# The feed-forward down projection of a decoder layer: seven products of half blocks in place of eight

## The reference, cut to what matters

```
y = (silu(c[..., :D_FF]) * c[..., D_FF:]) @ lp['ffn_w_down']    # 1056 x 2816 times 2816 x 1024
x = x + rms_norm(y, norm_g[5])                                  # over the 1024 columns of a row
```

## Time and profile before

| | |
|---|---|
| median of three runs | 3142.71 us (3140.87 to 3143.19) |
| span of the profiled execution | 3141.0 us |
| PE busy over the span | 2918.1 us (93%) |
| DVE, ACT, POOL busy | 1244.7, 631.2, 465.4 us |
| DMA | 345.05 MB, mean 110 GB/s |

### The profile page before, as it was taken

The page is one execution under the profiler, slowest core; times in us unless marked ns, Lnnn a source line. Parts: engine busy times, 40 slices in busy tenths (PEclk is TensorE's granted clock), DMA queues, the critical chain, the costliest instruction groups (busy, mean ns, idle before and its releaser), DMA issues. The chain is left out here.

```text
span 3141.0 us, 42970 instructions
## 1 busy us (share of the span) xinstructions
PE 2918.1 (93%) x15234; PEld 2006.5 (64%) x15234; DVE 1244.7 (40%) x2937; ACT 631.2 (20%) x1523; POOL 465.4 (15%) x349
## 2 busy tenths in 40 slices
PE   7999999998999788889999799998799999989998
PEld 5777777765666555456666566555588888864443
DVE  3111123233542567246666334233465655640000
ACT  2101100001222243134444211244211111110000
POOL 0000000003320333100000100011223333310100
PEclk8999999999999899989999899899899999999999
DMA  7544264426972542541111453300233334322110
GB/s 175 114 99 94 48 189 142 129 86 180 274 228 73 170 128 74 173 128 39 37 41 48 154 169 138 110 34 27 84 115 126 127 113 140 103 86 99 37 38 23
DMA packets 339366, 345.05 MB, mean 110 GB/s; under 512 B 61177, under 2 KB 310201, under 8 KB 337806
## 3 DMA queue, kind: packets, MB, share of 16 engines
q1 hardware_dynamic: 299458, 262.80, 29.1%
q10 hardware_dynamic: 39734, 79.98, 7.6%
HBM read 289.37 MB, written 110.01 MB: 127 GB/s over the span
## 5 line engine op out<-in xcount | busy, mean ns | idle before, releaser
L284 PE MATMUL d_ps<-d_w,mixer_u_T 128*128 128x288 f32 (+2 forms) x2048 | 585.5, 433 | 16.1 <-PEq L145 10.3
L284 PEld LDWEIGHTS d_ps<-d_w,mixer_u_T 128*128 128x128 f32 x2048 | 382.8, 194 | 157.0 <-issue 39.9
L288 PE MATMUL d_ps<-mixer_u_T,d_w 128*128 128x352 f32 x1152 | 402.6, 488 | 27.0 <-ACT d_ob L308 17.5
L2978 PE MATMUL down_ps<-down_w,feed_g_T 128*128 128x512 f32 x704 | 305.2, 596 | 8.4 <-DMA down_w<-ffn_w_down 8.4
L288 PEld LDWEIGHTS d_ps<-mixer_u_T,d_w 128*128 128x128 f32 x1152 | 212.2, 198 | 151.8 <-issue 70.6
L2978 PEld LDWEIGHTS down_ps<-down_w,feed_g_T 128*128 128x128 f32 x704 | 134.5, 191 | 177.5 <-issue 168.3
L3188 PE MATMUL ffn_ps<-up_u_T,up_up_w 128*128 128x264 f32 x704 | 164.6, 393 | 3.8 <-DMA ffn_state<-state_ffn_conv 3.8
L3188 PE MATMUL ffn_ps<-ffn_T,up_up_w 128*128 128x264 f32 x704 | 163.8, 386 | 0.0
L3188 PE MATMUL ffn_ps<-up_u_T,ffn_S 128*128 128x264 f32 x704 | 163.8, 386 | 0.0
L308 DVE COPY d_ob<-d_ps 128x288 f32<-128x288 f32 (+3 forms) x144 | 66.4, 462 | 244.2 <-PE d_ps L284 164.4
L3188 PEld LDWEIGHTS ffn_ps<-up_u_T,up_up_w 128*128 128x128 f32 x704 | 133.4, 192 | 26.9 <-issue 4.2
(11 more groups left out here) (493 smaller groups left out, 3740.5 us busy)
## 6 DMA issues: line engine op xcount, KB each, us to landing
out_dil_sample<-cache_dil_w ACTq DMA_DIRECT2D x10, 3264.0 KB
up_up_w<-ffn_w_up SPq DMA_DIRECT2D x44, 512.0 KB, 5.2
cmp_rows<-cache_nsa_kv SPq DMA_DIRECT2D x128, 128.0 KB
graw<-d_ob SPq DMA_DIRECT2D x72, 176.0 KB
mix_gate<-graw SPq DMA_DIRECT2D x24, 528.0 KB, 6.1
dils_qb<-proj SPq DMA_DIRECT2D x24, 512.0 KB, 7.3
d_w<-w_in SPq DMA_DIRECT2D x24, 512.0 KB, 5.6
ssd_x<-proj SPq DMA_DIRECT2D x29, 384.0 KB, 4.9
```

The costliest lines, as they stand in the source:

```text
L284: mm = pe.matmul(self.ps[u % 2][0:rows, 0:cols], self.u_T[:, k, r0:r0 + rows], self.view(i)[:, k, :], start=(k == 0), stop=(k == DK - 1))
L288: mm = pe.matmul(self.ps[u % 2][:, 0:cols], self.view(i)[:, k, x, :], self.u_T[:, k, c * third:(c + 1) * third], start=(k == 0), stop=(k = ...
L2978: mm = pe.matmul(ps[i % ring][:, 512 * h:512 * (h + 1)], lhs_T[:, k, r0:r0 + m], w[:, k, 512 * h:512 * (h + 1)], start=(k == 0), stop=(k = ...
```

## The change

The matrix of activations A (1024 tokens x 2816 features) and the weight B (2816 x 1024) are each seen as two by two blocks: A11 is the first 512 tokens by the first 11 feature blocks, B12 the first 11 feature blocks by the second 512 columns. Strassen's scheme in Winograd's form makes the four blocks of the product from seven block products instead of eight, with sums of blocks ahead of and behind them. A block product is 4 half products (one for each 128 tokens), each 11 matmuls of 128 x 512.

- DVE makes eight sums of blocks in place, each in two pieces of 5 and 6 feature blocks (L3102): in A21, A11, A12 and again A11; in B12 (twice), B11 and B21.
- PE's order is P1 into the four banks X, P2 into the banks Y, P5 into Y, P3 added onto P5 in Y, P6 added onto P1 in X, P4 into Y, P7 added onto X. The samples are multiplied with the whole, unchanged B inside P2, before the first sum in B.
- ACT copies P1, P5, P5+P3 and P4 out of PSUM (L3076, L3083, L3086, L3093), into `top`, into the freed block A21 and into the freed block B12. DVE adds the other part from PSUM to each (L3108, L3150, L3158, L3159), and the sum of squares is then taken from SBUF.
- The prompt tiles end in another order: tiles 0 to 3 behind P6, tiles 4 to 7 behind P7. Their residual rows are loaded into freed blocks behind P3.
- The weight comes in eight pieces of half rows (2 KB) instead of five of whole rows (4 KB).

More of the change, by code:

```diff
@@ L2907, in project_down, with after @@
 def project_down(nc, lhs_T, weight, gain_row, x_rows, out_rows, ident, rows_out):
[L2911 to L2914, removed]
+    KH, HALF, C, PAIRS = FFK // 2, D // 2, D // 4, PT // 2
+    SAMPLES = PT
+    EARLY = 5
+    ORDER = ([("P1", p) for p in range(PAIRS)] + [("P2", 0), ("P2", 1), ("P2", 2), ("samples", 0), ("P2", 3)]
+             + [(m, p) for m in ("P5", "P3", "P6", "P4", "P7") for p in range(PAIRS)])
+    OUTS_IN_ORDER = [SAMPLES] + list(range(PT))
+    n = len(OUTS_IN_ORDER)
+    def after(m, p=PAIRS - 1):
+        return ORDER.index((m, p)) + 1
     with Stage(nc, "down") as st:
@@ new lines, in quarters, with kept, bottom, x_of @@
+        def quarters(ap):
+            return ap.rearrange("p (a c) -> p a c", c=P)
+        def kept(part, p):
+            return A("A21", 4 * part, 4 * part + 4, P * p, P * (p + 1))
+        def bottom(p):
+            return w[:, 2 * p:2 * p + 2, HALF:D]
+        junk = A("A21", KH - 2, KH)
+        def x_of(t):
+            p = t % PAIRS
+            return A("A12", 2 * p, 2 * p + 2) if t < PAIRS else B("B22", 2 * p, 2 * p + 2)
+        def y_of(t):
+            return top[:, t] if t < PAIRS else bottom(t - PAIRS)
@@ L2935, in chunks, with halves @@
+        def halves(rows):
+            return rows.rearrange("t (a c) -> t a c", a=2)
         def chunks(rows):
             return rows.rearrange("t (c j) -> c t j", j=C)
[L2938 to L2944, removed]
         with nc.Block() as block:
@@ L2964, in _ @@
-                store(sp, n - 1)
-                for s in range(2):
-                    sp.wait_ge(stored[s], 16 * len(range(s, n, 2)))
+                sp.wait_ge(added, 1)
+                sp.dma_start(chunks(out_rows(SAMPLES)), y_s[:, :]).then_inc(stored, 16)
+                sp.wait_ge(product, after("P3"))
+                for t in range(PAIRS):
+                    sp.dma_start(x_of(t), halves(x_rows(t))).then_inc(xt_in, 16)
+                sp.wait_ge(T_made, 4)
+                for t in range(PAIRS, PT):
+                    sp.dma_start(x_of(t), halves(x_rows(t))).then_inc(xb_in, 16)
@@ L2968, in _ @@
+                for t in range(PT):
+                    sp.wait_ge(added, t + 2)
+                    sp.dma_start(halves(out_rows(t)), y_of(t)).then_inc(stored, 16)
+                sp.wait_ge(stored, 16 * n)
             @block.tensor
             def _(pe):
[L2970 to L2975, removed]
-                    else:
[L2977 to L2999, removed]
+                def half_product(bank, lhs, rhs, p, start):
+                    for k in range(KH):
+                        mm = pe.matmul(bank[:, :], lhs[:, k, P * p:P * (p + 1)], rhs[:, k, :], start=(start and k == 0), stop=(k == KH - 1), skip_group_check=not start)
+                    mm.then_inc(product, 1)
@@ new lines, in _ @@
+                for i in range(len(cuts["B11"]) - 1):
+                    pe.wait_ge(w_in["B11", i], 16)
+                    for k in range(cuts["B11"][i], cuts["B11"][i + 1]):
+                        for p in range(PAIRS):
+                            mm = pe.matmul(X[p][:, :], A("A11")[:, k, P * p:P * (p + 1)], B("B11")[:, k, :], start=(k == 0), stop=(k == KH - 1))
+                            if k == KH - 1:
+                                mm.then_inc(product, 1)
+                for i in range(len(cuts["B21"]) - 1):
+                    pe.wait_ge(w_in["B21", i], 16)
@@ new lines, in _ @@
+                for p in range(3):
+                    half_product(Y[p], A("A12"), B("B21"), p, True)
+                pe.wait_ge(w_in["B12", 0], 16)
+                pe.wait_ge(w_in["B22", 0], 16)
+                for k in range(FFK):
+                    for c in range(4):
+                        mm = pe.matmul(sample_bank[c * NS:(c + 1) * NS, 0:C], lhs_T[:, k, SEQ:TOK], w[:, k, c * C:(c + 1) * C],
+                                       start=(k == 0), stop=(k == FFK - 1))
+                mm.then_inc(product, 1)
@@ new lines, in _ @@
+                pe.wait_ge(S_made, 6)
[6 more added lines that the diff above has]
+                    half_product(X[p], A("A11"), B("B12"), p, False)
+                pe.wait_ge(T_made, 8)
+                for p in range(PAIRS):
+                    pe.wait_ge(held53, p + 1)
+                    half_product(later_bank(p), A("A22"), B("B21"), p, True)
@@ L3001, in _ @@
+                pe.wait_ge(S_made, 8)
+                for p in range(PAIRS):
+                    pe.wait_ge(c12, p + 1)
+                    half_product(X[p], A("A11"), B("B11"), p, False)
             @block.scalar
             def _(act):
[L3003 to L3009, removed]
@@ L3011, in root, with square @@
                 def root(i):
                     act.wait_ge(meaned, i + 1)
[L3013 to L3019 removed]
+                    act.activation(ss[:, 2, i:i + 1], ss[:, 1, i:i + 1], ACT.Sqrt).then_inc(rooted, 1)
+                def square(i, made, count):
+                    act.wait_ge(made, count)
+                    act.activation(junk, y_of(i - 1), ACT.Square, accum_out=ss[:, 0, i:i + 1]).then_inc(squared, 1)
+                    root(i)
@@ new lines, in _ @@
+                act.wait_ge(rows_out, 32)
+                for p in range(PAIRS):
+                    act.wait_ge(product, after("P1", p))
+                    act.copy(top[:, p, 0, :], X[p][:, :]).then_inc(held1, 1)
+                act.wait_ge(product, after("samples", 0))
+                act.activation(y_s[:, :], sample_bank[:, 0:C], ACT.Square, accum_out=ss[:, 0, 0:1]).then_inc(squared, 1)
+                root(0)
+                act.wait_ge(S_made, 4)
+                for p in range(PAIRS):
+                    act.wait_ge(product, after("P5", p))
+                    act.copy(kept(0, p), quarters(later_bank(p)[:, :])).then_inc(held5, 1)
@@ new lines, in _ @@
+                for p in range(PAIRS):
+                    act.wait_ge(product, after("P3", p))
+                    act.copy(kept(1, p), quarters(later_bank(p)[:, :])).then_inc(held53, 1)
+                for p in range(PAIRS):
+                    if p >= 1:
+                        act.wait_ge(squared, 1 + p)
+                    square(1 + p, c12, p + 1)
+                for p in range(PAIRS):
+                    act.wait_ge(product, after("P4", p))
+                    act.copy(bottom(p)[:, 0, :], later_bank(p)[:, :]).then_inc(held4, 1)
@@ L3028, in _ @@
                 dve.tensor_copy(fold[:, 1:4, :], fold[:, 0, :].unsqueeze(1).broadcast_to([P, 3, NS])).then_inc(folded, 1)
-                dve.wait_ge(gain_in, 80)
[L3030 to L3044, removed]
+                two(A("A21"), A("A21"), A("A22"), ALU.add, S_made)
@@ new lines, in _ @@
+                dve.wait_ge(S_made, 2)
+                dve.wait_ge(product, after("P1"))
+                two(A("A11"), A("A21"), A("A11"), ALU.subtract, S_made)
+                for p in range(3):
+                    corner(p)
+                dve.wait_ge(product, after("samples", 0))
+                two(B("B12"), B("B12"), B("B11"), ALU.subtract, T_made)
+                corner(3)
+                dve.wait_ge(totalled, 1)
+                dve.wait_ge(gain_in, 80)
+                scale(0, sample_bank[:, C:C + 1], y_s[:, :], sample_bank[:, 0:C], gain_c[:, :])
@@ new lines, in _ @@
+                dve.wait_ge(S_made, 4)
+                two(A("A12"), A("A12"), A("A11"), ALU.subtract, S_made)
+                dve.wait_ge(T_made, 2)
+                dve.wait_ge(product, after("P5"))
+                two(B("B12"), B("B22"), B("B12"), ALU.subtract, T_made)
+                dve.wait_ge(T_made, 4)
+                two(B("B11"), B("B12"), B("B11"), ALU.subtract, T_made)
+                two(B("B21"), B("B21"), B("B12"), ALU.subtract, T_made)
+                for p in range(PAIRS):
+                    dve.wait_ge(held53, p + 1)
+                    dve.wait_ge(product, after("P6", p))
+                    dve.tensor_tensor(quarters(top[:, p, 1, :]), kept(1, p), quarters(X[p][:, :]), ALU.add).then_inc(c12, 1)
+                    if p == PAIRS - 1:
+                        dve.wait_ge(S_made, 6)
+                        two(A("A11"), A("A22"), A("A11"), ALU.subtract, S_made)
+                    finish(p)
@@ L3048, in _ @@
                 clear(nc, pool)
[L3049 to L3053, removed]
+                pool.wait_ge(scaled, 1)
+                pool.wait_ge(xs_in, 16)
+                pool.tensor_tensor(y_s[:, :], y_s[:, :], x_s[:, :], ALU.add).then_inc(added, 1)
+                for t in range(PT):
+                    pool.wait_ge(scaled, t + 2)
+                    if t % PAIRS == 0:
+                        pool.wait_ge(xt_in if t < PAIRS else xb_in, 16 * PAIRS)
+                    pool.tensor_tensor(y_of(t), y_of(t), x_of(t), ALU.add).then_inc(added, 1)
 def load_up(eng, ins, w, w_in, m, slot):
```

77 lines of the change are left out of this document (52 added, 25 removed).

## The result

| | before | after |
|---|---|---|
| median, us | 3142.95 (3140.87 to 3146.71, 4 runs) | 3112.84 (3111.06 to 3113.27, 4 runs) |
| span of the profiled execution, us | 3141.0 | 3111.2 |
| the stage starts at, us | 2809.4 | 2814.8 |
| the stage lasts, us | 331.6 | 296.4 |

The ratio is 0.9899, with a 95% interval of 0.9886 to 0.9912 (the two medians alone give 0.9904). The forecast was 3107.2 us; the median lies 5.6 us above it and 0.3 us above the range. As a ratio to the 3142.7 us that it started from, the forecast is 0.9887, which lies inside the interval. The lower half of the table shows where the 5.6 us are. The stage is counted from the first semaphore clear that POOL issues at its head, 0.04 us ahead of the first transfer of the weight, to the end of the span. It became 35.2 us shorter, against 35.5 in the sum.

The account below looks back on a forecast made before the run. PE, busy throughout the stage, was taken as the bound: 3141.0 - 37.8 - 0.3 + 1.4 + 0.1 + 0.2 + 0.9 = 3105.5 us, plus 1.7 for the median gives 3107.2, range 3103.5 to 3112.5.

Parts of the forecast that it names:

- 44 matmuls, -37.8: On PE in the down stage: 44 of 352 matmuls go, at 0.858 us each, saving 37.8 us.
- 302.2, 9.7 and 2.4 us: PE's work in the stage before: 352 matmuls (302.2), the samples (9.7) and a slow start at the lower clock (2.4).
- Group borders and accumulation, nothing: On PE: accumulating onto a bank and a semaphore for every 11 matmuls instead of every 44 cost nothing.
- Eight sums of 6.2 us, all hidden: On DVE: eight block sums of 6.2 us, 49.5 us in all, hidden behind PE's work, least spare 3.6 us.
- first rival: The first sum in B12 is late for P5: 2.5 to 8.2 us, up to 2.4 more for PE's clock; 8%.
- The weight, nothing; the start, -0.3: Weight loads in half rows cost PE no wait; the smaller first piece starts PE 0 to 1.3 us sooner, 0.3 taken.
- third rival: The weight does not keep up: its pieces don't overlap, the samples wait some 46 us, total 3153 us; 2%.
- The end, +2.6: Behind the last matmul: two DVE adds +1.37, square and hand-over +0.1, store +0.2, 13 more semaphore clears +0.9 us.
- What would show it: Signs listed for the profile, among them about 12.4 us instead of 10.1 from the last matmul to the end.
- Its own upper bound: Whole kernel: the forecast's upper end without rivals, with nothing gained at the start, stated as 3108.6 us.
- Everything outside the stage is unchanged.: All stages ahead of the down projection: no change in time, so only the stage's terms are taken off 3141.0 us.
- 1.2 us either way: Whole kernel: the spread assumed for repeated runs, with a little more between chips, used for the range.

Follow-up runs that it names:

- before once more: The kernel before the change, run again with no edit: 3148.6 us, ratio 1.0001 to the kernel before.
- after once more: The changed kernel, run again with no edit: 3109.17 us, ratio 0.9876 to the kernel before.
- eight products again: The changed kernel with block product P4 multiplied twice, the first time for nothing: 3148.2 us, ratio 1.0006 to the kernel before.
- first sum late: The changed kernel with three unused 128 x 2048 subtractions on DVE ahead of the first sum in B12: 3114.11 us, ratio 0.9901 to the kernel before.
- first piece early: The changed kernel with B11's first two blocks loaded before the stage and sums in B cut at 2 blocks: 3104.53 us, ratio 0.9874.
- and a shorter end: Against the kernel with B11's first blocks loaded early: last tile's residual added on DVE, stage's semaphores left out of the clears; 3101.49 us.

## Why the prediction was right in the stage and short outside it

All eight profiles side by side, in us. The last column adds up, from the traces' records of the granted clock, how long the lower level was granted ahead of the stage.

| kernel | stage starts | stage lasts | lower level before it |
|---|---|---|---|
| before | 2809.4 | 331.6 | 218.5 |
| before once more | 2817.9 | 331.6 | 235.5 |
| after | 2814.8 | 296.4 | 228.7 |
| after once more | 2813.8 | 296.4 | 235.5 |
| eight products again | 2812.3 | 334.4 | 225.3 |
| first sum late | 2825.0 | 302.8 | 252.6 |
| first piece early | 2814.6 | 289.4 | 225.3 |
| and a shorter end | 2814.9 | 286.2 | 238.9 |

- **44 matmuls, -37.8.** Right: -37.4 from the first matmul to the engine behind the last, with 0.3 us more lost to the lower clock, and 38.0 when one product was put back. The prediction's 302.2, 9.7 and 2.4 us add up to 314.3 of the 314.8 that PE worked; the samples' fold is 0.3 of the rest, and the difference of the two kernels doesn't need it.
- **Group borders and accumulation, nothing.** Right: no idle time, and a granted clock of 1.00 in the three stretches shown, across groups of 22 instructions. The Trainium skill's rule on swings of the clock between groups ("TensorE: Matmul & The Clock Gate", section "A second HAM failure mode: psum-queue depth-cycling") has no case here: in the changed kernel's stage PE worked at the lower level only at its first matmuls, behind 7.9 us of idle time, and in the late-sum kernel once more behind 3.49 us, but not at borders without idle time.
- **Eight sums of 6.2 us, all hidden.** Right, with 3.5 us to spare at the first in B12 where 3.6 were worked out. PE's milestones from P1 to P7 came within 0.4 us of those worked out. The late sum showed that this cover is all there is at that place, and that the first rival was priced nearly right: 6.2 us where its terms give 5.8, since the clock cost 2.75 and not up to 2.4. The other sums were not made late.
- **The weight, nothing; the start, -0.3.** Right: the first matmul comes 6.16 us after the stage's start instead of 6.74, and 0.3 of that goes to the lower clock. The third rival's 46 us would have been some 39 by its own numbers, as the transfers are issued 6.7 us ahead of the first matmul.
- **The end, +2.6.** 2.8: adds 1.37, clears 0.92, and 0.5 for the store and the hand-overs, where 0.2 and 0.1 were taken. The "about 12.4 us" under "What would show it" doesn't fit the prediction's own terms, which give 10.1 + 2.6 = 12.7; 2.3 is the end less the 0.3 of the start. Its own upper bound is 3108.4 by its terms, not 3108.6.
- **"Everything outside the stage is unchanged."** This step failed. It holds for the code and not for the time of one execution: in two profiles of the same kernel before, the stage starts 8.5 us apart. The sum started from a profile whose first stages were the shortest of all eight, and that was luck: with the same 35.5 us taken off the median of the 23 later runs of before it would have given 3110.9.

A part of those microseconds can be seen in one stage of the mixer, on identical instructions (columns as in the stretches above); other stages ahead of the up projection add theirs. The kernel before, then the same kernel once more, then the late-sum kernel:

```profile
997.80:1303.40 305.60, 257.96 (x1132) 166.67 (x1132) 172.45 (x256) 94.31 (x199) 93.20 (x68) 0.93 0.39 116
```

```profile
1003.50:1311.90 308.40, 263.80 (x1132) 171.13 (x1132) 171.44 (x256) 94.39 (x199) 93.25 (x68) 0.91 0.38 115
```

```profile
1007.00:1318.20 311.20, 264.83 (x1132) 169.04 (x1132) 172.42 (x256) 94.42 (x199) 94.11 (x68) 0.91 0.38 114
```

The busy times of DVE, ACT and POOL agree within about 1%; PE's grows by 6 to 7 us at a lower granted clock, and the stage is 2.8 and 5.6 us longer, of 8.5 and 15.6 us by which the last stage starts later. The up projection, in which PE hardly waits, doesn't wander:

```profile
2234.00:2809.30 575.30, 566.80 (x2552) 476.44 (x2552) 344.03 (x602) 73.80 (x119) 168.84 (x178) 0.99 0.33 110
```

```profile
2239.50:2814.80 575.30, 566.81 (x2552) 476.51 (x2552) 344.00 (x602) 73.74 (x119) 168.75 (x178) 0.99 0.33 110
```

Before and after alike, 575.30 us. So the start wanders between executions of the same code by more than the 5.4 us, and the times of the changed kernel once more and of eight products leave no room for an effect of the change of that size. The time for which the lower level was granted goes with the wander: over the eight profiles the two have a correlation of 0.91, at some 0.4 us of start for each us at the lower level. That is a correlation; whether the lower level makes the waits or the waits bring the lower level was not separated, and what decides how much of it an execution gets is open.

The wander also makes the prediction's "1.2 us either way" too narrow: 23 runs of before on one chip spread by 20 us. Medians of four of them lie, in nine of ten cases, between 3.8 us below and 4.6 us above the median of all, so the range should have been wider by some 4 us on either side.

## What to carry to other kernels

Fewer products paid to the full here, where PE is busy without a break, and every block sum has a stretch of PE's work to hide behind. Find the one with the least cover, since a miss there cost its idle time and then a stretch at the lower clock. Compare versions by the stage's own length in the profile, which repeats to within 0.1 us here while the whole kernel wanders by several. What stays bare is worth a look once the bulk is hidden: loading 512 KB of the weight ahead and shortening the end made the stage 10 us shorter still.

## What the runs showed of the hardware

- The time of unchanged code ahead of the stage lay between 2809.4 and 2825.0 us in eight executions, and the shifts go with the time for which the lower clock level was granted ahead of it, 218.5 to 252.6 us (correlation 0.91). In the up projection, where PE is busy for 566.8 of 575.3 us, the length did not shift.
- After 3.49 us of idle time PE worked at the lower level for some 5 us of matmuls; after 1.53 us, in the kernel with the early piece, it stayed at the upper one (30 instructions in 13.14 us).
- A semaphore's clear at the kernel's end costs 0.07 us (0.92 us for 13 more).
- Sums on DVE of 128 x 2560 and 128 x 3072 float32 elements in SBUF took 2.82 and 3.35 to 3.48 us beside PE, and PE stayed busy for 50.00 of 50 us at a granted clock of 1.00.
